# A 512-column product split into two of 256 in the loop over heads, and its copy moved from VectorE to ScalarE

## The reference, cut to what matters

```python
p = jnp.einsum('btd,de->bte', h, w_in)          # h = rmsnorm(x, g_pre)
o_a = dilated_attention_prompt(q_a, k_a, v_a)   # three windows, 8 heads
o_b, conv_new, s_new = deltanet_branch(...)     # conv, SiLU, delta rule, 8 heads
y = jnp.einsum('bte,ed->btd', gated, w_out)
return x + rmsnorm(y, g_post)
```

## Time and profile before

| | us |
|---|---|
| median of 3 runs | 1197.86 |
| lowest and highest of them | 1197.4, 1198.62 |
| the profiled execution | 1204.32 |
| its span | 1202.5 |
| PE busy in the span | 1165.9 |
| PE weight loads busy | 1087.4 |
| DVE busy | 801.4 |
| ACT busy | 475.1 |
| POOL busy | 307.2 |

### The profile page before, as it was taken

One profiled execution on the slowest core, in us unless ns is written; L12 is line 12 of the kernel. 1 busy time (PEld: TensorE's weight loads), 2 busy tenths in 40 slices (PEclk: granted clock), 3 DMA queues, 4 the chain that ended last, 5 costly groups with the idle time before them and its releaser, 6 DMA issues. The chain is left out here.

```text
span 1202.5 us, 24731 instructions
## 1 busy us (share of the span) xinstructions
PE 1165.9 (97%) x8401; PEld 1087.4 (90%) x8401; DVE 801.4 (67%) x1987; ACT 475.1 (40%) x1216; POOL 307.2 (26%) x275
## 2 busy tenths in 40 slices
PE   5999999999999999999999999999999979999997
PEld 4899989998999899989988999899999979999996
DVE  5586567666766786777766766777776756565544
ACT  6453335434533444344434433453345335331211
POOL 0224112411242134122311241223122312222211
PEclk9999999999999999999999999999999999999999
DMA  7332455254525452635263525352535373423263
GB/s 249 93 98 73 145 158 162 72 165 147 168 64 177 136 162 62 203 110 166 67 193 108 168 66 194 116 161 81 182 111 168 93 251 129 150 88 101 73 212 143
DMA packets 83354, 164.18 MB, mean 137 GB/s; under 512 B 12801, under 2 KB 22882, under 8 KB 81698
## 3 DMA queue, kind: packets, MB, share of 16 engines
q1 hardware_dynamic: 81966, 161.47, 42.5%
q10 hardware_dynamic: 1312, 1.59, 0.5%
HBM read 144.78 MB, written 17.37 MB: 135 GB/s over the span
## 5 line engine op out<-in xcount | busy, mean ns | idle before, releaser
L643 PE MATMUL PJ<-h,w_hi 128*128 128x512 f32 x1110 | 419.3, 414 | 0.0
L1995 POOL TENSOR_TENSOR w_lo<-w_raw,w_hi 128x512 fp32r<-128x512 f32 x160 | 216.2, 1352 | 758.5 <-ACT w_hi L1035 758.1
L639 PE MATMUL PJ<-h,w_hi 128*128 128x264 f32 (+1 forms) x1216 | 358.0, 294 | 0.0
L640 PE MATMUL PJ<-h,w_hi 128*128 128x264 f32 (+1 forms) x1216 | 345.7, 284 | 0.0
L641 PE MATMUL PJ<-h,w_lo 128*128 128x264 f32 (+1 forms) x1216 | 345.4, 284 | 0.0
L644 PE MATMUL PJ<-h,w_lo 128*128 128x256 f32 x1110 | 311.3, 280 | 0.0
L643 PEld LDWEIGHTS PJ<-h,w_hi 128*128 128x128 f32 x1110 | 209.2, 188 | 42.8 <-DVE w_lo L1397 1.4
L640 PEld LDWEIGHTS PJ<-h,w_hi 128*128 128x128 f32 x1216 | 230.4, 189 | 2.2
L1035 ACT ACTIVATE w_hi<-w_raw 128x512 fp32r<-128x512 f32 x320 | 196.5, 623 | 86.4 <-PE PJ L641 79.1
L639 PEld LDWEIGHTS PJ<-h,w_hi 128*128 128x128 f32 x1216 | 230.0, 189 | 0.3
L641 PEld LDWEIGHTS PJ<-h,w_lo 128*128 128x128 f32 x1216 | 229.0, 188 | 0.0
(11 more groups left out here) (333 smaller groups left out, 1705.8 us busy)
## 6 DMA issues: line engine op xcount, KB each, us to landing
w_raw<-in_w_in SPq DMA_DIRECT2D x256, 256.0 KB, 2.7
w_raw<-in_w_out SPq DMA_DIRECT2D x64, 256.0 KB, 3.0
kvq<-in_cache_win_k SPq DMA_DIRECT2D x24, 512.0 KB, 5.0
kvq<-in_cache_win_v SPq DMA_DIRECT2D x24, 512.0 KB, 4.8
mem<-scratch_p SPq DMA_DIRECT2D x24, 512.0 KB, 5.7
out<-memx SPq DMA_DIRECT2D x16, 260.0 KB, 4.0
mem<-in_x_prompt SPq DMA_DIRECT2D x4, 1024.0 KB, 10.1
S<-in_state_delta SPq DMA_DIRECT2D x8, 512.0 KB, 5.8
```

Of the source, the lines that this page charges most:

```text
L639: pe.matmul(ps, wh, h_hi[:, k, tok], start=k == 0, stop=False)
L640: pe.matmul(ps, wh, h_lo[:, k, tok], start=False, stop=False)
L643: pe.matmul(both, wh, h2[:, :, k, tok], start=k == 0, stop=False)
L1995: pool.tensor_tensor(w_lo[:, par, 4 * q:4 * q + 4, :], w_raw[:, q, :, :], w_hi[:, par, 4 * q:4 * q + 4, :].bitcast(F32), ALU.subtract).the ...
```

## The change

In the loop over heads (tiles 2 to 64) half 0 is no longer wide. A step k of it becomes three products of 256 columns, as tile 1 has them, all into the same 256 columns of bank 0; the output tiles stay wide. So bank 0 holds one finished sum, and a plain copy takes it out: ACT's `copy_out`, in segment 5 (seg == 5, after ACT's step of that segment), where before DVE's `half_out` stood in segment 4. The waits of `guard` go with it from DVE to ACT. The semaphore `proj_half` is gone; PE waits for `proj_sb`, which each copy now raises by 1.

```diff
                 if q == 0 and not first:
-                    if half == 1 or out or isinstance(T, int) and T <= 2:
-                        pe.wait_ge(s["proj_sb"], made(T, half) - 2)
-                    else:
-                        pe.wait_ge(s["proj_half"], T - 2)
+                    pe.wait_ge(s["proj_sb"], made(T, half) - 2)
...
-                wide = half == 0 and not (isinstance(T, int) and T < 2)
+                wide = half == 0 and out
...
                     elif q == 0 and j == 0:
-                        pe.wait_ge(s["proj_sb"], 2 * T_O) if half == 1 else pe.wait_ge(s["proj_half"], T_O - 2)
+                        pe.wait_ge(s["proj_sb"], 2 * T_O - 1 + half)
...
             def copy_out(T, half, dst, off=0):
-                late = not (isinstance(T, int) and T < 2)
                 act.wait_ge(s["proj_ps"], made(T, half))
-                if late:
-                    act.wait_ge(s["proj_half"], T - 1)
...
-                    s["proj_sb"], 2 if late else 1)
+                    s["proj_sb"], 1)
...
                         step(work)
                         if seg % 2 == 0:
                             hi(T + 1, j % 2, seg // 2)
+                        if seg == 5:
+                            guard(h, j)
+                            copy_out(T, 0, *DST[j])
...
-            def half_out(h, j):
-                T = NT * h + (T_H + j)
-                dst, off = DST[j]
-                guard(h, j)
-                dve.wait_ge(s["proj_ps"], made(T, 0))
-                dve.tensor_reduce(dst[:, off:off + SPLIT], PJ[:, 0, :].rearrange("p (a t) -> p t a", a=2), AX.X,
-                                  ALU.add).then_inc(s["proj_half"], 1)
...
                     for seg in range(SEGS):
                         step(work)
-                        if seg == 4 and not (isinstance(h, int) and h == 0 and j == 0):
-                            half_out(h, j)
```

More of the change, by code:

```diff
@@ L341, in build @@
             "c_in ba_in g_in consts s_loaded x_sq rstd_ok x_scaled hT_ps h_hi_ok h_lo_ok st_ps st_sb memset_ok "
-            "w_hi_ok w_lo_dve w_lo_pool w_used proj_ps proj_half proj_sb "
+            "w_hi_ok w_lo_dve w_lo_pool w_used proj_ps proj_sb "
             "gates_pe gates_act gates_dve "
@@ L1065, in copy_out, with guard @@
                 act.activation(dst[:, o:o + WIDTH[half]], PJ[0:n, bank(T, half), 0:WIDTH[half]], ACT.Copy).then_inc(
-                    s["proj_sb"], 2 if late else 1)
+                    s["proj_sb"], 1)
             def guard_first():
                 act.wait_ge(s["cw_ok"], 1)
+            def guard(h, j):
+                if j == 0:
+                    act.wait_ge(s["scores"], NC * h)
+                    act.wait_ge(s["qkp"], h)
+                    act.wait_ge(s["q_row"], h)
+                elif j in (1, 2, 4):
+                    n = min(j, 3)
+                    act.wait_ge(s["conv_ok"], 3 * h + n)
+                    act.wait_ge(s["crow_out"], 16 * (3 * h + n))
+                elif j == 3 and (not isinstance(h, int) or h > 0):
+                    act.wait_ge(s["z_ok"], h)
+                elif j == 5:
+                    act.wait_ge(s["mix_qk"], h + 1)
+                    act.wait_ge(s["dkq"], h + 1)
+                elif j == 6:
+                    act.wait_ge(s["mix_T1"], 3 * h + 2)
+                    act.wait_ge(s["d_vec"], h + 1)
+                elif j == 7:
+                    act.wait_ge(s["z_ok_b"], h + 1)
             def stretch(h, before, work):
```

## The result

The kernel after takes 1207.13 us (median of 6 runs, 1205.52 to 1209.55), the kernel before beside it 1198.57 us (median of 6 runs, 1197.4 to 1200.67). The ratio is 1.0067, with a 95% interval of 1.0055 to 1.0079: the change makes the kernel slower by 8 us. The forecast was 1199.8, its range ended at 1203.9. The profiled execution of the kernel after took 1206.04 us, with a span of 1204.2.

The account below looks back on a forecast made before the run. PE was taken as the bound, busy 1165.9 of 1202.5 us and hardly waiting. Pace +2.0 us and three terms of 0 gave 1206.3 us against the profiled execution, scaled to a median of 1199.8 us, range 1195.4 to 1203.9.

Parts of the forecast that it names:

- DVE loses its copy: In the head loop, 63 DVE reductions, 43.2 us busy, go away; off PE's path while PE doesn't wait, worth 0.
- what is queued behind ACT's copy: On ACT, the making of w_hi for the next tile's segment 3, needed some 7 segments later: cost 0.
- slack of bank 0: At j = 0 and 2, ACT's later copy still leaves over 1 us before PE needs bank 0: cost 0.
- Pace: Half 0 of tiles 2 to 64: three short products take 352.5 ns a step against 350.5 wide, +2.0 us over 1008 steps.
- Weight loads: In half 0, 1008 more loads stay covered by the product ahead; each uncovered one would cost 0.083 us.
- sign of binding loads: In the profile after, half 0 product starts over 119 ns apart would mean the weight loads bind; 117 to 118 expected.
- These are the tightest of the eight tiles: Said of bank 0 at j = 0 and j = 2, where about 1 us of slack was read.
- bank 0 comes free late: Rival: ACT's copy comes late and PE waits half a microsecond in 16 tiles, +8 us; chance 0.10, shared with showing loads.
- first rival: One more late key load at a change of heads, where PE's slack is near zero: 3.7 us, 1203.5 us total; chance 0.15.
- The changes of heads: Between heads, the removed reduction precedes the key load's landing, so 0; one miss more or less is 3.7 us.

Follow-up runs that it names:

- e5: Kernel after with 70 already satisfied waits (35 instructions) added to DVE's stream, putting its later code back where it was: 1203.84 us, ratio 1.004 to before.
- e8: Kernel after with the third key block moved from the last tile into segments 1 and 2 of the next head: 1202.48 us, ratio 1.0023 to before.
- e7: Kernel before, products wide, with the third key block moved from the last tile into segments 1 and 2 of the next head: 1195.89 us, ratio 0.9976.
- e4: Kernel after, with ACT's copy in tile 7 of each head put behind the making of w_hi in segment 6: 1204.91 us, ratio 1.0047 to before.
- e6: Kernel before with 221 instructions of satisfied waits in DVE's first head, so later code lies relative to 256-instruction boundaries as in after: 1203.74 us, ratio 1.004.
- e9: Kernel after with ACT's copy in segment 4 in the first head, segment 6 in other heads' tile 7, and 70 satisfied waits on DVE: 1200.56 us, ratio 1.0009.
- e10: Kernel after with the three repairs of e9 and the third key block in segments 1 and 2 of the next head: 1197.18 us, ratio 0.9984 to before.
- e2: Kernel before, products still wide, with DVE's reduction of half 0 an eighth later, in segment 5 instead of 4: 1213.04 us, ratio 1.011.
- e3: Kernel after with ACT's copy in segment 4 instead of 5: 1205.09 us, ratio 1.0041 to before.

## Why the prediction was wrong

Two terms that stood at 0 failed: the place of DVE's code ("DVE loses its copy") and what is queued behind ACT's copy. The first is the largest, and without it the measured median would have stayed within the range: with the stall padded away (e5) the ratio is 1.0040 (up to 1.0054 by its interval), and the range ended at 1203.9 / 1197.86 = 1.0050. The slack of bank 0 in the first head and the size of the pace add the rest.

**Pace: right in kind, 1.3 us too small.** The forecast took 352.5 ns against 350.5 for a step, 2.0 ns. The runs give 3.3 ns (e8 against e7), at 1008 steps +3.3 us, within the 0 to +4 that stood as its range. Of its rows the long run of 264 columns came nearest: by the other way of scaling, which stood beside it (353.1), the difference would have been 2.6. The short stretches of 256 columns told nothing. The steps themselves show where it was off. Of those in the loop between 160 and 960 us with no other product in them and under 400 ns, the wide ones of before average 350.1 ns (477 of them), as forecast, the short ones of after 354.5 (532), 2.0 more than the 352.5 taken. Half 1 gives a little back, for a reason not known: 362.9 ns before, 362.2 after (591 each).

**Weight loads: no lost cover.** In half 0 the starts are 118.2 ns apart (354.5 / 3), under the 119 named as the sign of binding loads. Whether the 4.4 ns that a step takes longer are the third load or a fixed part of a product, no run tells apart. Half 1 of an output tile runs as before, 15 steps in 5.44 us, 121 ns a product:

```profile
1065.57 0.29 PE L636 MATMUL PJ<-h,w_hi 128*128 128x264 f32 x1
...
1071.01 0.29 PE L636 MATMUL PJ<-h,w_hi 128*128 128x264 f32 x1
```


**Bank 0 in the heads of the loop: right.** The slack at j = 0 and j = 2 is 1.19 and 1.24 us, where the prediction read about 1.0 us and over 1 us. **In the first head: wrong.** "These are the tightest of the eight tiles" was read from one head of the loop. The first head has the gates besides, in ACT's queue ahead of the copy, and there PE waited 1.17 us. The rival "bank 0 comes free late" named the mechanism, but for 16 tiles with 8 us; it was one tile.

**What is queued behind ACT's copy: a step that failed.** The prediction said "needed some 7 segments later: cost 0". PE indeed needs these weights only then. But w_hi has another reader first: POOL makes w_lo of it at once, and DVE's key block, then gB, can't pass POOL. The engine on which an operation is moved was followed to its next user on PE, and not to the one on POOL whose operation holds DVE. Behind 0.26 us on ACT came 0.23 us a head on PE, 1.6 us in all (e4, which undoes this alone, is 0.20% or 2.4 us under after). That PE's slack for gB "is near zero" stood in the first rival, which gave it 0.15 of the chances and thought of one miss of 3.7 us, not of a small one each time.

**The changes of heads in before weren't free either.** The earlier trace rows counts three waits; by e7 the third key block cost 0.32 us at each change of heads, most of it not seen as a wait.

**The output phase: the largest failed step.** 4.1 us, the largest single part, came from DVE's stream being 35 instructions shorter (3.2 us by the medians of e5 and after, 4.1 by e6). "None of this is on PE's path ... so it is worth 0", said of DVE's copy, looked at its time and not at its code. No row of the profile of before shows what another length would do; that stalls for "issue" could come and go with the length of a stream would have been a rival of +4 us, with its mirror for a stall that goes.

**DVE's relief: open.** e9 and e10 are about 2 us faster than the pace alone would make them, but no profile shows that DVE's lighter load is the cause.

**By the runs**: pace 3.3, gB 1.6, first head 1.2, code place 3 to 4: 9 to 10 us, of which about 2 are missing in e9 and e10 for a cause that isn't shown. Measured are 8.56, by the interval 6.6 to 9.5.

**Open.** Why the fetch comes late at that boundary and not at the others: in the five kernels with the stall the loads' queue fills the DMA engines around the packet (98 to 103% of them over 1 us), around the fetch at 1045.10 in before 74%, around that at 1034.24 in e5 8%. That fits, but it wasn't tried apart. And why the key load came late once in the profiled execution of before, which cost it 3.7 us with the clock: no change of heads in the profiles of the experiments loses as much.

## What to carry to other kernels

When an operation is put ahead of another on an engine, follow every reader of what it delays, on all engines, up to one that has no slack; in this kernel a product's due time was 7 segments away and another engine's was a quarter of a microsecond away. Where VectorE and GpSimd both work from SBUF, a GpSimd operation ahead of VectorE's urgent work can be on the critical path too. And when a change lengthens or shortens an engine's stream, look in the profile after for idle stretches that end by "issue" in code that wasn't touched, and undo them by padding before judging the change: some 4 of the 8 us here came from the length of a stream and not from the new order of work.

## What the runs showed of the hardware that was not expected

- VectorE's operation with two inputs in SBUF, begun beside a GpSimd subtraction, ended 0.15 us behind that one in the three rows shown (0.80, 0.43 and 1.37 us instead of 0.28). A VectorE operation with one input of 128x4 was held too, for 1.26 us instead of 0.17 (e2).
- An instruction fetch stopped VectorE for 3.03 to 3.31 us in five kernels (after, e3, e4, e6 and e8), each at the same instruction of the output phase, with an 8 KB fetch packet 1.74 to 1.78 us before it went on; 35 satisfied-wait instructions more moved the stall away (e5), 221 more brought it to the kernel before (e6).
- At the same 768 columns, three products of 256 in fp32r with three weight loads take 354.5 ns, two products of 512 and 256 with two loads 350.1; by the distance of heads the loop loses 3.3 ns a step (e8 against e7), 0.9%.
